# Sums over partitions from high and low parts in a two-block transformer kernel

## The reference

```python
v = sc_b * causal_dwconv(sc_c * sc_u, sc_conv_w)
y_sc = grouped_rmsnorm(v, sc_norm, SC_GROUPS)            # 16 groups of 128 features

o = rmsnorm_2(o, subln_g, SUBLN_EPS) * (1.0 - lam_init)   # differential heads, 8 of width 128

log_1m_beta = jnp.where(causal, -jax.nn.softplus(z), 0.0)  # stick-breaking heads, 8 of width 64
suffix = lax.cumsum(log_1m_beta, axis=3, reverse=True) - log_1m_beta
a = jnp.where(causal, jnp.exp(jax.nn.log_sigmoid(z) + suffix), 0.0)
o = rmsnorm_2(o, head_g[:, None, :])                      # the same norm in the 8 banded heads
```

## Time and profile before

| | |
|---|---|
| median of 3 runs | 2714.44 us (2714.43 to 2728.66) |
| span of the profiled execution | 2712.9 us (no other time of that execution is given; the median is 1.5 above the span) |
| TensorE busy, matmuls | 2692.4 us, 99% |
| TensorE weight loads | 2328.4 us, 86% |
| VectorE busy | 1945.3 us, 72% |
| ScalarE busy | 1300.5 us, 48% |
| granted TensorE clock, mean | 0.999 |
| read from HBM | 496.93 MB, 185 GB/s over the span |

### The profile page before, as it was taken

How to read it: one execution, slowest core, us unless ns; L and a number is a source line. 1 busy time by engine, 2 the same in 40 slices (tenths; PEclk the granted TensorE clock), 3 DMA queues, 4 the chain that set the end, 5 groups by cost and what they waited for, 6 DMA issues and landing times.

```text
span 2712.9 us, 37271 instructions
## 1 busy us (share of the span) xinstructions
PE 2692.4 (99%) x15234; PEld 2328.4 (86%) x15234; DVE 1945.3 (72%) x2414; ACT 1300.5 (48%) x1655; POOL 94.3 (3%) x68
## 2 busy tenths in 40 slices
PE   8999999999999999999999999999999999999998
PEld 7888888888898888888888888888888888888887
DVE  7777888986868665666566785777787757775775
ACT  5444556755545443444344544645544433443444
POOL 1000000012101000000000120000000000000000
PEclk9999999999999999999999999999999999999999
DMA  6555555456556655555556555454555665565554
GB/s 242 192 184 185 178 171 176 147 177 215 187 171 195 214 190 191 187 192 188 192 182 192 195 175 182 148 168 151 179 179 194 192 194 180 186 202 193 177 193 158
DMA packets 139769, 501.47 MB, mean 185 GB/s; under 512 B 15424, under 2 KB 18256, under 8 KB 139344
## 3 DMA queue, kind: packets, MB, share of 16 engines
q1 hardware_dynamic: 136512, 491.41, 55.3%
q10 hardware_dynamic: 3088, 7.70, 0.8%
HBM read 496.93 MB, written 3.68 MB: 185 GB/s over the span
## 4 chain that ended last, share of the span: by engine, by line
PE 92%; DVE 4%; ACT 2%; issue 1%; DMA 1%; POOL 0%; DVEq 0%; ACTq 0%; POOLq 0%
PE PS L515 92%; DVE wlo L1293 2%; ACT whi L862 1%; DVE AR L1641 1%; DVE XG L1504 0%; DVE AR L1415 0%; DMA raw<-in_w_in 0%; ACT AR L968 0%; ACT L847 0%; DVE AR L1422 0%; POOL AR L1866 0%; DVE AR L1276 0%; DVE H L1287 0%; DVE AR L1431 0%; DMA XG<-in_x 0%
## 5 line engine op out<-in xcount | busy, mean ns | idle before, releaser
L515 PE MATMUL PS<-H,whi 128*128 128x512 f32 x5072 | 1783.3, 397 | 10.1 <-DVE wlo L1809 7.2
L1293 DVE TENSOR_TENSOR wlo<-raw,whi 128x1024 fp32r<-128x1024 f32 x929 | 1131.3, 1235 | 605.3 <-ACT whi L862 604.2
L862 ACT ACTIVATE whi<-raw 128x1024 fp32r<-128x1024 f32 x929 | 973.2, 1057 | 951.0 <-PE PS L515 865.0
L515 PE MATMUL PS<-H,wlo 128*128 128x256 f32 x5072 | 1412.0, 278 | 0.0
L515 PEld LDWEIGHTS PS<-H,whi 128*128 128x128 f32 x5072 | 953.0, 188 | 235.5 <-DVE H L1287 7.2
L515 PEld LDWEIGHTS PS<-H,wlo 128*128 128x128 f32 x5072 | 955.9, 188 | 2.5 <-issue 1.9
L515 PE MATMUL PS<-Y,whi 128*128 128x512 f32 (+1 forms) x1408 | 473.5, 387 | 0.9 <-DVE XG L1777 0.6
L515 PE MATMUL PS<-Y,wlo 128*128 128x256 f32 x1344 | 373.9, 278 | 0.0
L515 PEld LDWEIGHTS PS<-Y,whi 128*128 128x128 f32 x1408 | 260.0, 188 | 58.4 <-issue 1.7
L515 PEld LDWEIGHTS PS<-Y,wlo 128*128 128x128 f32 x1344 | 253.1, 188 | 0.3
L515 PE MATMUL PS<-whi,Y 128*128 128x512 f32 x704 | 216.9, 389 | 0.0
(11 more groups left out here) (196 smaller groups left out, 1085.8 us busy)
## 6 DMA issues: line engine op xcount, KB each, us to landing
raw<-in_ffn SPq DMA_DIRECT2D x528, 512.0 KB, 4.5
raw<-in_w_in SPq DMA_DIRECT2D x177, 512.0 KB, 4.5
raw<-in_w_qkv SPq DMA_DIRECT2D x96, 512.0 KB, 3.7
raw<-in_w_out SPq DMA_DIRECT2D x64, 512.0 KB, 4.4
raw<-in_w_o SPq DMA_DIRECT2D x40, 512.0 KB, 3.6
raw<-in_w_q SPq DMA_DIRECT2D x8, 512.0 KB, 3.6
raw<-in_w_k SPq DMA_DIRECT2D x8, 512.0 KB, 3.6
raw<-in_w_v SPq DMA_DIRECT2D x8, 512.0 KB, 4.1
```

What stands on the lines that cost most here:

```text
L515: return e.matmul(out, l, r, start=start, stop=stop)
L862: a.then_inc(e.activation(c.whi[:, s % NW, :], c.raw[:, s % NRAW, :], ACT.Copy), "whi")
L1293: v.then_inc(e.tensor_tensor(c.wlo[:, s % NW, :], c.raw[:, s % NRAW, :], c.whi[:, s % NW, :].bitcast(F32), ALU.subtract), "wlo")
```

## The change

The sum of squares of the gated convolution, the sums of the heads' norms and the running sums of the stick-breaking heads are no longer made from float32 operands. The operand is split into a high part in fp32r, by ScalarE, and a low part in fp32r, which VectorE makes by a subtraction; TensorE multiplies the fp32r copy of ones (or `tri2`, or the block matrix `bd`) with each and adds them in one bank. The parts lie in places of Y that are free at that time. The sum's wait is now for the semaphore of the low part (`sc_lo`, `dif_y`, `stk_y`, `bnd_y`, `stk_m`). stk and bnd are changed like dfb:

```diff
     def sc(j):                                  # TensorE
         yield from idle(9)
         bank = take("sc", j, "b")
-        p.wait_ge("sc_sq", j + 1)
-        p.then_inc(mm(bank, c.ones, c.sc_q[j % 2], True, True), "sc_sum")
+        p.wait_ge("cr", 5)
+        p.wait_ge("sc_lo", j + 1)
+        mm(bank, c.ones_r, c.sc_h, True, False)
+        p.then_inc(mm(bank, c.ones_r, c.sc_l, False, True), "sc_sum")
...
     def dfb(h):                                 # TensorE
...
         yield from idle(2)
         bank = take("dfb", h, "n")
-        p.wait_ge("dif_sq", h + 1)
-        p.then_inc(mm(bank[:, 0:T], c.ones, q[:, 0:T], True, True), "dif_n")
+        p.wait_ge("dif_y", 2 * h + 1)
+        mm(bank[:, 0:T], c.ones_r, c.hi("Y", h), True, False)
+        p.then_inc(mm(bank[:, 0:T], c.ones_r, c.lo("Y", h), False, True), "dif_n")
...
     def stk(i):                                 # TensorE, step 10, n over two lanes
-            p.wait_ge("stk_m", 2 * i + n + 1)
-            mm(bank[:, 0:256], TRI2, q[:, 0:256], True, False)
-            mm(bank[:, 128:256], c.ones, q[:, 256:384], False, True)
-            p.then_inc(mm(bank[:, 256:384], TRI2, q[:, 256:384], True, True), "stk_c")
+            p.wait_ge("stk_m", 4 * i + n + 3)
+            mm(bank[:, 0:256], c.tri2_r, qh[:, 0:256], True, False)
+            mm(bank[:, 0:256], c.tri2_r, ql[:, 0:256], False, False)
+            mm(bank[:, 128:256], c.ones_r, qh[:, 256:384], False, False)
+            mm(bank[:, 128:256], c.ones_r, ql[:, 256:384], False, True)
+            mm(bank[:, 256:384], c.tri2_r, qh[:, 256:384], True, False)
+            p.then_inc(mm(bank[:, 256:384], c.tri2_r, ql[:, 256:384], False, True), "stk_c")
...
     def sc(j):                                  # ScalarE, step 4
         a.wait_ge("sc_v", j + 1)
+        a.wait_ge("sc_sum", j) if j else None
+        a.then_inc(e.activation(c.sc_h, v, ACT.Square))
         a.then_inc(e.activation(q, v, ACT.Square), "sc_sq")
...
+    def square_pair(src, hi, q, sem):           # ScalarE, in dfb, stk and bnd
+        a.then_inc(e.activation(hi, src, ACT.Square))
         a.then_inc(e.activation(q, src, ACT.Square), sem)
...
     def stk(i):                                 # ScalarE
-        yield from idle(8)
+        yield from idle(4)
+        for n in range(2):
+            a.wait_ge("stk_m", 4 * i + n + 1)
+            a.wait_ge("stk_c", 2 * i) if i else None
+            a.then_inc(e.activation(c.stk_h[n], lanes[n][1][:, 0:384], ACT.Copy), "stk_ln")
+        yield from idle(4)
...
     def sc(j):                                  # VectorE
-        yield from idle(12)
+        yield from idle(6)
+        v.wait_ge("sc_sq", j + 1)
+        v.then_inc(e.tensor_tensor(c.sc_l, q, c.sc_h.bitcast(F32), ALU.subtract), "sc_lo")
+        yield from idle(6)
...
     def dfb(h):                                 # VectorE
         q = c.dif[h % 4][1]
-        yield from idle(4)
+        yield from idle(2)
+        v.wait_ge("dif_sq", h + 1)
+        v.then_inc(e.tensor_tensor(c.lo("Y", h), q[:, 0:T], c.hi("Y", h).bitcast(F32), ALU.subtract), "dif_y")
+        yield from idle(2)
         v.wait_ge("dif_root", h + 1)
...
     def stk(i):                                 # VectorE, after the masks of step 7
-        yield from idle(4)
+        yield from idle(2)
+        for n in range(2):
+            v.wait_ge("stk_ln", 4 * i + n + 3)
+            v.then_inc(e.tensor_tensor(c.stk_l[n], lanes[n][1][:, 0:384], c.stk_h[n].bitcast(F32), ALU.subtract), "stk_m")
+        yield from idle(2)
...
     def cr(_):                                  # VectorE
+        v.then_inc(e.tensor_copy(c.ones_r, c.ones), "cr")
```

More of the change, by code:

```diff
@@ L248 @@
     "dfa": [("s0", 2, 4, "dif_max", 2, 1), ("s1", 2, 4, "dif_max", 2, 2), ("t", 8, 9, "dif_copy", 1, 1)],
-    "dfb": [("o", 0, 5, "dif_y", 1, 1), ("n", 2, 4, "dif_root", 1, 1)],
+    "dfb": [("o", 0, 5, "dif_y", 2, 2), ("n", 2, 4, "dif_root", 1, 1)],
     "stk": [("s0", 2, 4, "stk_q", 2, 1), ("s1", 2, 4, "stk_q", 2, 2), ("c0", 10, 12, "stk_z", 2, 1),
-            ("c1", 10, 12, "stk_z", 2, 2), ("o", 16, 21, "stk_y", 1, 1), ("n", 18, 20, "stk_root", 1, 1)],
+            ("c1", 10, 12, "stk_z", 2, 2), ("o", 16, 21, "stk_y", 2, 2), ("n", 18, 20, "stk_root", 1, 1)],
     "bnd": [("s0", 2, 4, "bnd_max", 2, 1), ("s1", 2, 4, "bnd_max", 2, 2), ("t0", 9, 11, "bnd_copy", 2, 1),
-            ("t1", 9, 11, "bnd_copy", 2, 2), ("o", 12, 17, "bnd_y", 1, 1), ("n", 14, 16, "bnd_root", 1, 1)],
+            ("t1", 9, 11, "bnd_copy", 2, 2), ("o", 12, 17, "bnd_y", 2, 2), ("n", 14, 16, "bnd_root", 1, 1)],
 }
@@ L411, in __init__ @@
         self.grp_q = [M[3], M[4]]
+        self.sc_h, self.sc_l = self.pair("Y", 14), self.pair("Y", 15)
+        last = self.op["Y"][:, 13:16, :, :].rearrange("p a b c -> p (a b c)")
+        self.stk_h, self.stk_l = ([last[:, o:o + 384] for o in at] for at in ((0, 384), (768, 1152)))
         self.xa_p = [G[4], G[5], M[3], M[4]]
@@ L673, in dfb @@
     def dfb(h):
-        V, WT, q = c.V["a"], c.dif[h % 4][0], c.dif[h % 4][1]
+        V, WT = c.V["a"], c.dif[h % 4][0]
         bank = take("dfb", h, "o")
@@ L697, in stk @@
         yield from idle(8)
-        TRI2 = c.const2("tri2")
+        p.wait_ge("lam_v", 4)
         for n in range(2):
-            q = lanes[n][1]
+            qh, ql = c.stk_h[n], c.stk_l[n]
             bank = take("stk", i, f"c{n}")
-            p.wait_ge("stk_m", 2 * i + n + 1)
-            mm(bank[:, 0:256], TRI2, q[:, 0:256], True, False)
-            mm(bank[:, 128:256], c.ones, q[:, 256:384], False, True)
-            p.then_inc(mm(bank[:, 256:384], TRI2, q[:, 256:384], True, True), "stk_c")
+            p.wait_ge("stk_m", 4 * i + n + 3)
[5 more added lines that the diff above has]
+            p.then_inc(mm(bank[:, 256:384], c.tri2_r, ql[:, 256:384], False, True), "stk_c")
         yield from idle(6)
@@ L717, in stk @@
         bank = take("stk", i, "n")
-        p.wait_ge("stk_sq", i + 1)
-        p.then_inc(mm(bank[:, 0:T], c.const2("bd"), lanes[0][1][:, 0:T], True, True), "stk_n")
+        p.wait_ge("stk_y", 2 * i + 1)
+        mm(bank[:, 0:T], c.bd_r, c.hi("Y", 8 + i), True, False)
+        p.then_inc(mm(bank[:, 0:T], c.bd_r, c.lo("Y", 8 + i), False, True), "stk_n")
         yield
@@ L753, in bnd @@
         bank = take("bnd", i, "n")
-        p.wait_ge("bnd_sq", i + 1)
-        p.then_inc(mm(bank[:, 0:T], c.const2("bd"), q[:, 0:T], True, True), "bnd_n")
+        p.wait_ge("bnd_y", 2 * i + 1)
+        mm(bank[:, 0:T], c.bd_r, c.hi("Y", 12 + i), True, False)
+        p.then_inc(mm(bank[:, 0:T], c.bd_r, c.lo("Y", 12 + i), False, True), "bnd_n")
         yield
@@ L1055, in dfb @@
         a.wait_ge("dif_pv", h + 1)
-        gained_square(c.bank("dfb", h, "o")[:, 0:T], q[:, 0:T], "dif_sq")
+        square_pair(c.bank("dfb", h, "o")[:, 0:T], c.hi("Y", h), q[:, 0:T], "dif_sq")
         yield from idle(2)
@@ L1061, in dfb @@
         yield from idle(2)
-        a.wait_ge("dif_y", h + 1)
+        a.wait_ge("dif_y", 2 * h + 2)
         a.then_inc(e.activation(c.hi("Y", h), q[:, 0:T], ACT.Copy), "y_hi")
@@ L1090, in stk @@
         a.wait_ge("stk_pv", i + 1)
-        gained_square(c.bank("stk", i, "o")[:, 0:T], q[:, 0:T], "stk_sq")
+        square_pair(c.bank("stk", i, "o")[:, 0:T], c.hi("Y", 8 + i), q[:, 0:T], "stk_sq")
         yield from idle(2)
@@ L1115, in bnd @@
         a.wait_ge("bnd_pv", i + 1)
-        gained_square(c.bank("bnd", i, "o")[:, 0:T], q[:, 0:T], "bnd_sq")
+        square_pair(c.bank("bnd", i, "o")[:, 0:T], c.hi("Y", 12 + i), q[:, 0:T], "bnd_sq")
         yield from idle(2)
@@ L1568, in stk @@
         yield from idle(3)
+        if i == 0:
+            v.then_inc(e.tensor_copy(c.bd_r, c.const2("bd")))
         v.wait_ge("y_made", made("ao", 5 if i == 0 else 7 if i == 1 else 6 + i))
@@ L1592, in stk @@
             v.then_inc(e.tensor_tensor(z, z, CM, ALU.mult), "stk_a")
-        yield from idle(6)
+        yield from idle(4)
         q = lanes[0][1]
+        v.wait_ge("stk_sq", i + 1)
+        v.then_inc(e.tensor_tensor(c.lo("Y", 8 + i), q[:, 0:T], c.hi("Y", 8 + i).bitcast(F32), ALU.subtract), "stk_y")
+        yield from idle(2)
         v.wait_ge("stk_root", i + 1)
@@ L1628, in bnd @@
                 v.then_inc(e.tensor_scalar(Pb[:, o:o + w], Pb[:, o:o + w], st[:, 4 + k:5 + k], None, ALU.mult), "bnd_w" if k else None)
-        yield from idle(9)
+        yield from idle(7)
+        v.wait_ge("bnd_sq", i + 1)
+        v.then_inc(e.tensor_tensor(c.lo("Y", 12 + i), q[:, 0:T], c.hi("Y", 12 + i).bitcast(F32), ALU.subtract), "bnd_y")
+        yield from idle(2)
         v.wait_ge("bnd_root", i + 1)
```

12 lines of the change are left out of this document (6 added, 6 removed).

## The result

| | before | after |
|---|---|---|
| median | 2714.69 us (2714.43 to 2728.66) | 2762.62 us (2760.55 to 2777.49) |
| ratio, 95% interval | | 1.0185 [1.0168, 1.0203] |
| span of the profiled execution | 2712.9 us | 2758.9 us |
| granted clock, mean | 0.999 | 0.994 |

The kernel is slower by 48 us. The forecast was 32 us; its own range ended at 2757, the range over all cases at 2764. Profile against profile it is 46.0 us. Some executions of most kernels here, of the kernel before too, lie 14 us above the rest, and where a median or a profile holds such a one the text says so.

The account below looks back on a forecast made before the run. TensorE, busy 99% of the span, was taken as the bound; new waits of 40.3 us less 7.9 us of saved work gave +32.4, so 2747 us at 65%, own range 2736 to 2757, over all cases 2726 to 2764.

Parts of the forecast that it names:

- work saved on TensorE: Conv, norm and running sums: fp32r pairs cost less than float32 sums, taking 7.9 us off TensorE, at most 9.5.
- stops, heads: Differential heads' norm sums: TensorE waits for VectorE's low part, queued behind the next head's softmax, at seven heads; 22.3 us.
- stops, stk norm, running sums, bnd: Waits for low parts at stick-breaking norm sums 8.3 us, running sums 4.6, banded heads' norm sums 3.5, with releases.
- stop, first conv sum: Gated convolution: only the first of eight sums waits, for the copy of ones and the subtraction; 1.6 us with release.
- half clock behind the stops: TensorE after the new stops: clock stays at full speed, no drop counted, 0 us.
- a granted clock below 1.0 between 1680 and 1930 us: Profile after, in that stretch: the sign that would show the waits come and the clock falls at long stops.
- rival (b): Waits come and the clock falls at each of five stops of 3 us or more: 11.5 us more, 2758; 15%.
- Rival (a): New waits don't appear, low halves are in time and only the savings remain: 2706.5 us; 8%.
- (c): Waits are real but half as long, each stop letting VectorE catch up for the next: +12, 2727 us; 8%.
- Rival (d): Short-format pairs save nothing, two weight loads and passes costing what the float32 sum did: 2755 us; 4%.
- The added work: About 17 us more on VectorE and some 14 on ScalarE, covered by their spare time and costing nothing as throughput.

Follow-up runs that it names:

- the heads alone: Kernel before with only the norm sums of the eight differential heads (dfb) changed to pairs; 2750.89 us, ratio 1.0116.
- the filler: Kernel after with unneeded matmuls added on TensorE ahead of the differential, stick-breaking norm and running sums' waits (eight, or five at running sums); 2751.70 us, ratio 1.0129.
- the work alone: Kernel after, high and low parts still made, but sums float32 and waiting for the squares as before; 2714.93 us, ratio 0.9995.
- float32 conv sums: Kernel after with all low parts made earlier, but the gated convolution's sums float32 at step 9 as in the kernel before; 2711.94 us, ratio 0.9988.
- low part one step earlier: Kernel after with VectorE making the differential heads' low part at step 1 in place of 2; 2745.26 us, ratio 1.0096.
- the kernel after once more: Kernel after, unchanged, measured and profiled a second time; 2763.73 us, span 2761.9 us.
- before with the added sum: Kernel before with one unused float32 sum of 256 columns on TensorE, 12 slots into the first feed-forward part; 2715.09 us, ratio 0.9994.
- conv sums alone: Kernel before with only the gated convolution's sums (sc) and the copy of ones changed; 2714.38 us, ratio 0.9997.
- all low parts earlier: Kernel after with low parts one to four steps ahead of sums, some sums a step later, copy of ones earlier; 2711.79 us, ratio 0.9992.

## Why the prediction was wrong

The sum against its own profile, term by term:

| | forecast | measured |
|---|---|---|
| work saved on TensorE | -7.9 | -7.7 |
| stops, heads (with the old 1.1 us wait gone) | 22.3 | 20.6 |
| stops, stk norm, running sums, bnd | 16.4 | 15.7 |
| stop, first conv sum | 1.6 | 1.0 |
| half clock behind the stops | 0 | 14.0 |
| before's own drop at 1596 us, absent | 0 | -1.6 |
| slower blocks between conv sums | 0 | 1.9 |
| rest: pairs behind a stop 1.2, other small delays | 0 | 2.1 |
| sum | 32.4 | 46.0 |

**The failed step is the clock.** The prediction said "TensorE's granted clock stays at full speed all through, also over its present short gaps" and "I count no drop in the forecast". It counted a drop for none of its twenty stops; nine had one, at 1.55 us each (14.0 us by the starts of the blocks that fall into them). Its own sign of this, a granted clock below 1.0 between 1680 and 1930 us, came: 0.91 over 1680 to 1800 and 0.95 over 1800 to 1900. Both the heads alone (clock low only where stops are) and the filler (11 us back with eight drops fewer) tie them to the stops. Without this term the sum is 32 us, the forecast's; that it meets it so closely is partly luck, since stops 3.0 us shorter than forecast and the old drop's absence are made up for by the slower blocks and the rest.

The claim was false already in the kernel before, in a stretch that the prediction didn't open. It has a stop of 2.1 us that begins at 1593, and the windows over it and behind it read:

```profile
1592.00:1596.00 4.00, 1.89 (x11) 1.40 (x10) 3.86 (x5) 3.81 (x5) 3.11 (x2) 1.00 0.24 55
1596.00:1600.00 4.00, 4.00 (x15) 3.37 (x14) 4.00 (x3) 1.35 (x2) 2.10 (x2) 0.57 0.52 164
```

Fifteen matmuls start in four microseconds where 23 do at full clock. This one row shows that 2.1 us can be enough, and its price, 1.6 us; with it a term for the clock would have stood in the forecast, as it does in rival (b). I took instead the one long gap at the very end, 3.9 us, for the length from which a drop comes, though such a row only says that 3.9 was enough. The mean clock of 0.999 hid it: one drop is a thousandth of the span. Rival (b), at 15%, had the mechanism; it counted only the five stops of 3 us and more and priced them at 2.3 us from the start of the kernel. Its 11.5 us come near the 14.0 by luck: too few drops, each too dear.

The Trainium skill, "TensorE: Matmul & The Clock Gate", section "Why this matters for your kernels", advises no idle gap above about 3 us between bursts. The profiles agree above 3 us (eight of eight stops had a drop) and show drops below it, behind new stops of 1.6 to 2.4 us, eight times in the two profiles of the kernel after; the measurement decides.

**The waits were right**, in place, order and nearly in size: seven heads, none at head 7, longest 4.35 us at head 6 (forecast 4.5), norm sums of stk 8.7 with releases (8.3), running sums 4.2 (4.6), bnd 2.8 (3.5). Head 1's is 2.4 against 3.0 us. Rival (a), no waits, and (c), half the waits, fell. **The savings were right**: a pair over 512 columns costs 0.47 for 0.86, a pair over 256 costs 0.24 for 0.43, and a lane's running sums save 0.19, from start to start in the kernels in which no pair waits: 3.1, 3.1 and 1.5 us. Behind a stop that no drop follows a pair over 256 costs 0.31 to 0.35, some 1.2 us more for fifteen, which the sum did not have. Rival (d) falls with these pitches. **The added work is free**, as "the work alone" showed. What the reading of the conv stage missed is the blocks' pitch, 1.9 us of its 3.1.

With the stops gone, part of the saving is still missing: over the attention part the kernel with float32 conv sums gains 2.4 us against before, not the 4.6 of its pairs, in one like profile. The softmax's transposes cost 0.9 us more in all, other side steps 0.3, and the remaining 1.0 lies in the blocks between them. By my reading VectorE's low parts now stand ahead of the softmax; that was not tried by itself.

## What to carry to other kernels

When a sum is handed from one engine to two, count the steps between the last maker and the consumer by where each engine's own queue stands at that step, not by the step's number; one or two steps more of lead were worth 50 us here at no change of work. When a change makes a busy TensorE stop, open the windows behind every stop that the kernel already has, and price the drop of the clock from them; a mean clock of 0.999 doesn't say that there is none. A format that makes a small operation cheaper is worth its saving only after the stops are out, and here no more than half of it arrived even then.

## What the runs showed of the hardware

**A drop of the clock is not a function of the stop's length.** The same stops of the same program (2.0 to 2.4 us) had one in one execution and none in the next; in the profile of "low part one step earlier" none of the six stick-breaking stops up to 2.2 us had one. The old stop that begins at 1593 us in before is in all fourteen profiles, 2.1 us long in each; six have a drop behind it (before, the work alone, low part one step earlier, the kernel after once more, float32 conv sums, and before with the added sum), eight have none. What decides, no run here shows.

**The main stream has two paces.** Blocks follow each other at 0.347 or at 0.353 us (0.3467 and 0.3533; my texts rounded the second to 0.354), and a pace set behind a side operation holds until the next one. After float32 conv sums all stretches were at 0.347; after pairs every third at 0.353, and in the second profile of the kernel after all eight. The matmuls started in 30 us tell them apart, first of the kernel after behind conv sums 0 and 1, then of its second profile:

```profile
62.00:92.00 30.00, 30.00 (x172) 26.03 (x171) 23.04 (x28) 14.35 (x17) 0.00 (x0) 1.00 0.58 200
96.00:126.00 30.00, 30.00 (x175) 26.47 (x174) 21.96 (x27) 13.45 (x16) 0.00 (x0) 1.00 0.56 192
```

```profile
96.00:126.00 30.00, 30.00 (x172) 25.99 (x171) 21.36 (x25) 13.56 (x16) 0.00 (x0) 1.00 0.56 184
```

96 blocks x 6.6 ns x 3 stretches are the 1.9 us of the table. The executions that are 14 us longer are the same thing on 2109 blocks that no side operation interrupts, behind a sum that waits for GpSimd: at 0.353 in the three profiles that are such executions (conv sums alone, low part one step earlier, all low parts earlier), at 0.347 in the other eleven. The same 720 us in the profile of "all low parts earlier" (an upper execution), then with one sum put in 12 slots after:

```profile
840.00:1560.00 720.00, 720.00 (x4077) 624.37 (x4077) 460.55 (x461) 303.61 (x320) 5.65 (x4) 1.00 0.58 189
```

```profile
840.00:1560.00 720.00, 720.00 (x4156) 629.80 (x4155) 472.14 (x474) 311.02 (x329) 8.51 (x6) 1.00 0.59 192
```

4156 to 4077 is 1.019, as 0.3533 to 0.3467 is; 2109 x 6.6 ns is 13.9 us. With a sum of 0.43 us in the running stream the upper group was absent from 35 executions, where a fifth of them would be seven. The kernel with float32 conv sums had none in 11 either, without it, which chance allows. What sets the pace, I don't know.
